# The loop-closing jumps of PE, ACT and DVE in an expert loop are announced at the loop head

## What is computed

```python
combine = jnp.sum(jax.nn.one_hot(top_idx, N_EXPERTS) * top_w[..., None], axis=1)
y = jnp.zeros_like(t)
for e in range(N_EXPERTS):
    hid = jax.nn.silu(t @ w_gate[e]) * (t @ w_up[e])
    y = y + combine[:, e:e + 1] * (hid @ w_down[e])
```

## Time and profile before

| | us |
|---|---|
| runs | 2001.38, 2008.28, 2009.51 |
| median | 2008.28 |
| the profiled execution, its own time | 1999.2 |
| its span, first to last instruction | 1997.5 |
| start of the expert loop in it | about 862 |
| jumps back in it (DVE) | 1173.3, 1448.5, 1702.2 |
| last iteration leaves the loop (DVE) | 1977.4 |

### The profile page before, as it was taken

How to read it: one execution, slowest core, us unless ns; L and a number is a source line. 1 busy time by engine, 2 the same in 40 slices (tenths; PEclk the granted TensorE clock), 3 DMA queues, 4 the chain that set the end, 5 groups by cost and what they waited for, 6 DMA issues and landing times.

```text
span 1997.5 us, 21265 instructions
## 1 busy us (share of the span) xinstructions
PE 1773.3 (89%) x8790; PEld 960.5 (48%) x8791; DVE 508.5 (25%) x938; ACT 163.3 (8%) x340; POOL 2.5 (0%) x9
## 2 busy tenths in 40 slices
PE   5897999999999999969788879899889888798994
PEld 2346888688888864444322243322242222432221
DVE  0522536655445011320211110211201111111114
ACT  0000013100000000130000010000020000200000
POOL 0000000000000000000000000000000000000000
PEclk8998999999999999989999989999989999899997
DMA  9888774687766544306689986899979999598995
GB/s 394 356 323 289 299 322 192 257 344 295 323 275 277 220 190 168 139 31 253 242 334 427 425 347 274 337 426 427 427 299 427 426 425 428 209 368 364 427 426 219
DMA packets 49256, 630.68 MB, mean 316 GB/s; under 512 B 5615, under 2 KB 8080, under 8 KB 10152
## 3 DMA queue, kind: packets, MB, share of 16 engines
q1 hardware_dynamic: 47512, 621.58, 75.3%
q10 hardware_dynamic: 1552, 6.57, 0.8%
HBM read 624.46 MB, written 3.67 MB: 314 GB/s over the span
## 4 chain that ended last, share of the span: by engine, by line
PE 75%; DMA 14%; DVE 4%; issue 4%; SPq 2%; ACT 1%; ACTq 0%; DVEq 0%
PE bank L750 38%; PE bank L552 23%; PE bank L563 9%; DMA ring<-in_w_down 6%; DMA ring<-in_w_up_gate 4%; PE bank L575 2%; DMA region_a<-in_x_T 2%; DMA ring<-in_w_in 1%; DMA ring<-in_ada_w 1%; SPq L409 1%; DVE region_a L1577 1%; PE bank L570 1%; DVE ada_rows L1286 1%; PE bank L620 0%; PE bank L783 0%
## 5 line engine op out<-in xcount | busy, mean ns | idle before, releaser
L552 PE MATMUL bank<-ring,region_b 128*64 128x512 f32 x2048 | 479.2, 622 | 67.6 <-issue 54.8
L750 PE MATMUL bank<-region_a,ring 128*128 128x256 f32 x1792 | 393.5, 381 | 12.6 <-DMA ring<-in_w_in 12.6
L750 PEld LDWEIGHTS bank<-region_a,ring 128*128 128x128 f32 x1792 | 341.7, 191 | 62.9 <-DMA ring<-in_w_in 13.0
L552 PEld LDWEIGHTS bank<-ring,region_b 128*64 128x64 f32 x2048 | 148.6, 143 | 372.3 <-issue 364.0
L563 PE MATMUL bank<-ring,region_f 128*64 128x512 f32 (+1 forms) x1536 | 258.7, 524 | 30.6 <-DMA ring<-in_w_down 24.3
L1286 DVE SCALAR_TENSOR_TENSOR ada_rows<-ring,condT,ada_rows 128x512 f32<-128x512 f32 x293 | 220.3, 752 | 10.4 <-DMA ring<-in_ada_w 0.5
L563 PEld LDWEIGHTS bank<-ring,region_f 128*64 128x64 f32 (+1 forms) x1536 | 87.3, 128 | 186.9 <-issue 136.4
L1577 DVE TENSOR_TENSOR region_a<-bank,region_a 128x512 f32<-128x512 f32 x128 | 79.5, 684 | 259.6 <-PE bank L575 258.7
L750 PE MATMUL bank<-ring,region_a 128*128 128x512 f32 x256 | 119.9, 626 | 6.2 <-DVE region_a L1263 6.2
L750 PE MATMUL bank<-ring,region_b 128*128 128x512 f32 x256 | 110.3, 592 | 1.3 <-issue 1.3
L750 PE MATMUL bank<-region_e,region_x 128*128 128x256 f32 x256 | 65.2, 422 | 30.8 <-DVE region_e L1622 30.8
(11 more groups left out here) (165 smaller groups left out, 669.6 us busy)
## 6 DMA issues: line engine op xcount, KB each, us to landing
ring<-in_w_up_gate SPq DMA_DIRECT2D x128, 2048.0 KB, 17.6
ring<-in_w_down SPq DMA_DIRECT2D x64, 2048.0 KB, 15.6
ring<-in_ada_w SPq DMA_DIRECT2D x48, 2048.0 KB, 13.1
ring<-in_w_in SPq DMA_DIRECT2D x34, 2048.0 KB, 17.5
ring<-in_w_branch SPq DMA_DIRECT2D x8, 2048.0 KB, 17.6
ring<-in_w_out SPq DMA_DIRECT2D x8, 2048.0 KB, 11.3
ring<-in_w_in SPq DMA_DIRECT2D x4, 1024.0 KB, 4.9
region_a<-in_x_T ACTq DMA_DIRECT2D x4, 512.0 KB, 26.4
```

The costliest lines, as they stand in the source:

```text
L552: last = nc.tensor.matmul(bank_of(x, j)[n * c:n * c + n, 0:2 * m], tokens(x, 8 * half + k), w[:, k, :, m * c:m * c + m], start=(half == 0 ...
L750: return nc.tensor.matmul(out, lhsT, rhs, start=start, stop=stop)
```

## The change

```diff
             pe.wait_ge(routed, 1)
-            with pe.Fori(0, NE // GRP) as g:
+            with nc.Fori(0, NE // GRP, engines=[mybir.EngineType.PE], hint_back_edge=True) as g:
...
             act.wait_ge(routed, 1)
-            with act.Fori(0, NE // GRP) as g:
+            with nc.Fori(0, NE // GRP, engines=[mybir.EngineType.Activation], hint_back_edge=True) as g:
...
-            with dve.Fori(0, NE // GRP) as g:
+            with nc.Fori(0, NE // GRP, engines=[mybir.EngineType.DVE], hint_back_edge=True) as g:
```

## The result

| | before | after |
|---|---|---|
| runs shown at first, median | 2008.28 (3 runs) | |
| all runs measured together, median | 2000.42 (9 runs) | 1988.66 (9 runs) |
| ratio after / before, 95% interval | | 0.9936, 0.9917 to 0.9954 |
| profiled execution, own time / span | 1999.2 / 1997.5 | 1988.66 / 1985.5 |
| mean granted clock over the span | 0.955 | 0.957 |

The change makes the kernel faster by 0.64%, which is 12.8 us of 2000.42 (9.2 to 16.6); the two medians alone are 11.8 us apart. The three runs that the forecast started from had a median 7.9 us above that of the nine.

The account below looks back on a forecast made before the run. Matmuls and the weight stream alternate as the bound, except at three jumps back, where DVE ends last. Gain 15.8 - 0.75 - 0.2 = 14.8 us, less 4.3 at the end, is 10.5: from 2008.3 to 1997.8 us, range 1993 to 2000.

Parts of the forecast that it names:

- DVE's gap: Idle time behind DVE's three jumps back, 15.8 us in sum, was to shrink to 0.75 us.
- PE's gap: PE's own 5.98 us at its jump, hidden behind DVE by 3.5 us, was to go too.
- The announcement itself: One added instruction per iteration, on the path on DVE alone: 0.2 us for three, bounds 0 and 0.1 each.
- Does the gain reach the end: Behind each gather the weight ring is full, so matmuls and transfers move 5 us earlier and nothing is given back.
- The clock: Low clock at the gather's start stays about as long: 0 us, bounds +1 and -2.5 us.
- The last iteration: Where DVE's jump isn't taken, the last LayerNorm's code comes late: 4.3 us lost, between 0 and 5.25.
- The base: Start of the count: the 2008.3 us median of the runs, though the profiled execution lay 9 us below it.
- no stall at the end: Rival: all of the forecast without the loss behind the loop, 14.8 us gained, 1993.5 us; chance 0.17.
- the end term: The 4.3 us taken off the gain for DVE's late code behind the loop; 0.5 to 5.25 in the range.
- The announcement does nothing: Rival: all gaps at the jumps stay, 2008.3 us plus 0.2; chance 0.23, including only PE's or DVE's working.
- Slower: Rival: early fetching of the loop head stops PE mid-body, 5.98 us in each of four iterations, 2021.7 us; chance 0.08.

Follow-up runs that it names:

- the version with the tiles ahead: Against the kernel before, DVE writes the next iteration's hot tiles during the fourth expert, and all three jumps are announced; ratio 0.9892, median 1983.09 us.
- the run made for it: Changed kernel with DVE's loop head shifted and four semaphore increments added, so a piece of program ends right behind DVE's closing branch; ratio 0.9971.

## Why the prediction was right or wrong

*DVE's gap*: right in kind, and sized 0.2 us too well. Behind the branch 0.47 us are left in place of the 0.25 us taken from SP's row at each jump, the larger part of the step from 14.8 us to the 14.0 measured at the three. The 108 ns that the Trainium skill gives for a compare-and-branch ("Advanced Engine Details and Errata", Control Flow Timing) lie above DVE's branch rows, 74 to 85 ns, and far below PE's taken and announced branch, 364 ns.

*PE's gap*: right, and shown by two runs. DVE's was the one that ended last, PE's own would have allowed a gather 6.0 us after the scatter, and 6.1 us was measured with DVE's jump alone announced.

*The announcement itself*: 0.04 us, inside its bounds.

*Does the gain reach the end*: right. The gather starts 4.66 us earlier each time. The step's sign, a silence of DMA 5 us shorter, came in the first profile only at the second jump (8.26 to 3.64 us); the other two silences, 17 us, stayed as long, and both have the low clock behind the gather in them. In the second profile of the changed kernel, which lacks that low clock, all three are shorter: 13.1, 3.3 and 13.5 us against 17.2, 8.3 and 17.1 before.

*The clock*: right for this change. The first gather ran 5.7 us at 1.2 GHz (1172.29 to 1178.0), the second 3.9 and the third 5.2, against 4.5, 5.9 and 4.8 before. Its bound of -2.5 us would not have held for a gather that starts at once: in the version with the tiles ahead the low stretch is gone and 2.2 to 2.9 us of each gather with it, 7.4 us in three, which comes back behind the gather.

*The last iteration*: this step failed. I took 4.3 us for the code behind the loop and measured no gap. The premise held in the run made for it, an announced jump that falls through leaves the next code to be fetched late, but there the visible stall is 1.7 us, and in the changed kernel nothing of it shows. I priced it by the gap of a taken jump, 5.25 us, and allowed one or two operations to cover it. Laid bare, the next code was there 3.0 us behind the branch, and in the changed kernel the cover was whole.

*The base*: the larger error, and the second step that failed. I had noted that the profiled execution lay 9 us below the median and still counted from the median of three runs, 2008.28 us; the median of nine is 2000.42.

So "no stall at the end" was the right case, though its 1993.5 us is 4.8 us too high as well; the base makes the difference. It has 14.8 us gained at the jumps, the profiles show 14.0, and the runs give 12.8 and 13.6 us (0.64% and 0.68%). Against the forecast of 1997.8 us, 1988.66 us lies 9.1 us lower: 7.9 from the base and 4.3 from the end term, less 3.0, because the medians are 11.8 us apart and not 14.8. The forecast's range was also narrower than its own bounds: with 0.5 us at the end and 2.5 us from the clock it reaches down to 1991.5 us and not to 1993, which is still above the result.

From the profile's own 1999.2 us the gain of 10.5 gives 1988.7. That this meets the result is partly luck: the 4.3 us wrongly taken off made the forecast too high, and the low clock behind two gathers made this execution slower by about as much. The second profiled execution, without it, took 1984.15 us.

"The announcement does nothing" fell with the first row after. "Slower", by stops in the middle of PE's body, did not occur: PE's fetches became three fewer, and no new kind of "issue" stands inside the iterations (57.2 us before L552 in 12 waits, 54.8 in 12 before). The rule of the Trainium skill's "Runtime: NRT & Kernel Launch", Instruction fetch mechanics, that prefetch is purely sequential, doesn't hold where a jump is announced early: by it the 5 to 6 us would have stayed.

## What to carry to other kernels

A jump back over a long body cost here 5.0 to 6.6 us per iteration on each engine whose program had to come in again. Announce it at the head on every engine at once: the slowest of them decides, so one engine alone gave part or nothing, and an announcement next to the jump gave nothing. Then look at what stands between the last work of one iteration and the first of the next, since moving it ahead of the jump took the ratio from 0.9936 and 0.9932 to 0.9892 here, some 8 us more. Expect a part of that back: when the work at the head starts at once, the next wait shows, here 3.6 us behind each gather, 2.2 us more than the wait that was there. Where the weight stream is the bound, faster jumps bought nothing, however much PE waited for "issue" there.

## What was not expected of the hardware

Each announced jump made one fetch of program fewer on PE (117 to 114 pieces for three jumps), and 103 pieces with the experts' jumps announced too. An announced jump that isn't taken cost 1.7 us behind the branch in the one run made to show it, and nothing visible in the others. An announcement 59 us ahead of the jump, but with only 43 rows of the trace between on DVE and 16 on ACT, bought nothing. A gather that follows the scatter within 0.5 us ran at 2.4 GHz throughout, while after 4.6 us of standing still it began with 1.2 GHz. And where DVE's loop lies in its program may matter by itself, which isn't shown: shifted by a few instructions, with DVE's jump not announced, the kernel was 0.4% slower in one case (1.0040, 1.0018 to 1.0061); the other case, 1.0018 (0.9995 to 1.0041), is not told apart from none.
